# Threshold search shared between two engines: ScalarE counts the two longest tiles, in step with the projection

## The reference

```python
rel = jax.nn.relu(jnp.einsum('bthd,bsd->bths', qi, ki))
score = jnp.einsum('bths,bth->bts', rel, wi) * idx_scale
score = jnp.where(allowed[None], score, -jnp.inf)
top_val, top_idx = lax.top_k(score, topk)          # topk = 256
logits = einsum(q, k[top_idx]) * HEAD_DIM ** -0.5
p = jax.nn.softmax(logits)
out = einsum(p, v[top_idx])
```

## Time and profile before

| | |
|---|---|
| median of 3 runs | 1478.3 us |
| the profiled execution | 1476.31 us |
| its span | 1474.4 us |
| PE busy | 1288.4 us (87%) |
| DVE busy | 911.0 us (62%) |
| ACT busy | 638.5 us (43%) |
| POOL busy | 436.5 us (30%) |
| 224 counts on DVE (L1750) | 214.5 us, and 17.3 us for reading their sums |
| POOL's rows between 500 and 550 us | none |

### The profile page before, as it was taken

The page is one execution under the profiler, slowest core; times in us unless marked ns, Lnnn a source line. Parts: engine busy times, 40 slices in busy tenths (PEclk is TensorE's granted clock), DMA queues, the critical chain, the costliest instruction groups (busy, mean ns, idle before and its releaser), DMA issues.

```text
span 1474.4 us, 29883 instructions
## 1 busy us (share of the span) xinstructions
PE 1288.4 (87%) x10636; PEld 925.0 (63%) x10636; DVE 911.0 (62%) x1691; ACT 638.5 (43%) x1253; POOL 436.5 (30%) x518
## 2 busy tenths in 40 slices
PE   5968788999995336788997999999999998999997
PEld 3443334544443225566444888888888887888887
DVE  4324679999999995898655655555555553222012
ACT  3546786544156314887333444444444442101011
POOL 4772336486297100000202333333333310000001
PEclk9988999999997558999999999999999999999999
DMA  5221000102112100100531222222222128121013
GB/s 192 87 62 32 15 27 19 58 36 92 62 29 63 37 1 15 44 31 24 155 123 37 59 57 57 57 57 57 57 57 57 28 79 210 44 79 37 0 30 90
DMA packets 81594, 86.67 MB, mean 59 GB/s; under 512 B 6768, under 2 KB 63120, under 8 KB 81520
## 3 DMA queue, kind: packets, MB, share of 16 engines
q1 hardware_dynamic: 76112, 75.07, 17.8%
q10 hardware_dynamic: 4848, 8.99, 1.6%
q0 software_dynamic: 560, 1.61, 0.4%
HBM read 72.34 MB, written 13.31 MB: 58 GB/s over the span
## 4 chain that ended last, share of the span: by engine, by line
PE 51%; DVE 6%; ACT 2%; issue 2%; DMA 1%; SPq 1%; POOL 0%; POOLq 0%; DVEq 0%; ACTq 0%
PE PS L1139 28%; PE PS L1196 14%; PE PS L1102 5%; DVE M L1858 2%; DVE M L1847 2%; DMA M<-in_w_down 1%; PE PS L1022 1%; PE PS L1052 1%; PE PS L999 1%; SPq L631 1%; PE PS L1183 1%; ACT M L1454 0%; PE PS L1116 0%; ACT M L1443 0%; DVE M L425 0%
## 5 line engine op out<-in xcount | busy, mean ns | idle before, releaser
L1139 PE MATMUL PS<-M 128*128 128x264 f16 x3696 | 420.0, 277 | 9.6 <-ACT M L1562 9.6
L1139 PEld LDWEIGHTS PS<-M 128*128 128x128 f16 x3696 | 363.2, 98 | 66.0 <-ACT M L1562 10.2
L873 PE MATMUL PS<-M 128*128 128x512 f16 (+1 forms) x1512 | 305.9, 363 | 3.9 <-DVE M L425 3.6
L1196 PE MATMUL PS<-M 128*128 128x256 f16 x2112 | 233.0, 274 | 6.2 <-DVE M L2080 6.2
L873 PEld LDWEIGHTS PS<-M 128*128 128x128 f16 (+1 forms) x1512 | 138.7, 103 | 154.1 <-issue 13.8
L1196 PEld LDWEIGHTS PS<-M 128*128 (+1 forms) x2112 | 207.1, 98 | 31.7 <-issue 7.1
L1750 DVE TENSOR_SCALAR_CACHE_REDUCE M<-M,small 128x384 f16<-128x384 f32 (+6 forms) x224 | 214.5, 987 | 0.4 <-DVE small L1762 0.3
L667 POOL TENSOR_TENSOR small<-small 128x1 f32<-128x1 f32 x27 | 5.5, 203 | 543.1 <-ACT M L1509 293.7
L821 POOL TENSOR_TENSOR M<-M 128x264 f32<-128x264 f32 x44 | 34.7, 789 | 282.6 <-ACT M L1562 282.6
L2080 DVE SCALAR_TENSOR_TENSOR M<-PS,M 128x256 f32 (+1 forms) x32 | 13.6, 424 | 164.6 <-PE PS L1196 164.5
L1919 DVE SCALAR_TENSOR_TENSOR M<-M 128x2048 f16<-128x2048 f32 (+1 forms) x44 | 88.9, 2024 | 36.2 <-ACT M L1500 36.2
(11 more groups left out here) (167 smaller groups left out, 1860.3 us busy)
## 6 DMA issues: line engine op xcount, KB each, us to landing
M<-in_w_in SPq DMA_DIRECT2D x24, 512.0 KB, 4.5
M<-in_w_gate SPq DMA_DIRECT2D x22, 512.0 KB, 4.0
M<-in_w_up SPq DMA_DIRECT2D x22, 512.0 KB, 5.2
M<-in_w_down SPq DMA_DIRECT2D x20, 512.0 KB, 4.0
M<-in_x_prompt SPq DMA_DIRECT2D x16, 512.0 KB, 4.8
M<-in_w_out SPq DMA_DIRECT2D x8, 512.0 KB, 3.8
h_scratch<-M ACTq DMA_DIRECT2D x8, 512.0 KB, 5.1
M<-h_scratch SPq DMA_DIRECT2D x16, 256.0 KB, 7.3
```

Of the source, the lines that this page charges most:

```text
L873: last = pe.matmul(bank(b)[:, 0:w], xnT[:, ds(t, 1), k, s, :].squeeze(1), wt[wbuf(c)][:, k * w:(k + 1) * w], start=(k == 0 and i == 0), st ...
L1139: last = pe.matmul(o, wsp[x][:, zw, wb, k * P:(k + 1) * P], ablk[:, ab, za, k * HT + s * SC:k * HT + (s + 1) * SC], start=(name not in kep ...
L1196: last = pe.matmul(o[:, 0:256], cols[:, ds(m * SC + r * P, P)], wt[dc % 2][:, f, :], start=(f == 0 and i == 0), stop=(f == FT - 1 and i == 2))
```

## The change

Of each round's seven counts, the two of the longest tiles (7 and LAST) move to ACT. There the threshold minus the score goes through Sign, the signs are summed, and a tiny copy makes a count of the sum (`sign_count`). The first of these stands behind E, the second at the end of a step, in 31 steps: all of u, k and v and four of q. Tile 7 gets 32 more columns, filled with an inadmissible value, so that both are 1056 wide. DVE counts five tiles, waits for ACT (`act_counted`), and judges and turns bits for all seven at once; its loops become straight code, and the `piece_lo` stand singly behind rounds. Ties count half by signs, so two counts and four tiny steps at the end set these two thresholds exactly. The scratch of the masks moves to the rows that the counts dump into, and four of the seven masks follow the search at once, without waiting for q; the other three stay before jobs 1, 3 and 5.

```diff
+            def sign_count(c, t, i):
+                b = round_of(c, t)
+                j = ON_DVE + i
+                o = SC_OFF[SCORE_TILES[j]]
+                if i == 0:
+                    act.wait_ge(sel, b * SEL_ROUND + (SEL_FIRST - SEL_ROUND))
+                else:
+                    act.wait_ge(signs_summed, b * ON_ACT - 1)
+                act.activation(sign_out, scores[:, o:o + TOK], ACT.Sign, scale=-1.0, bias=kth[:, j:j + 1],
+                               accum_out=signs[:, i:i + 1]).then_inc(signs_summed, 1)
+                if i == ON_ACT - 1:
+                    act.wait_ge(signs_summed, b * ON_ACT)
+                    act.activation(cnt[:, ON_DVE:NS], signs, ACT.Copy, scale=-0.5, bias=TOK / 2).then_inc(act_counted, 1)
...
                     E(c, t, rep)
+                    if searching(c, t):
+                        sign_count(c, t, 0)
...
+                    if searching(c, t):
+                        sign_count(c, t, 1)
...
-        EARLY_MASKS = 0
+        EARLY_MASKS = 4
...
-        tie = [view(RW, oX + 4608 * i + 1024, [TOK], F16) for i in range(2)]
+        tie = [d[:, 0:TOK] for d in dump]
...
+            def bit_round(b):
+                base = SEL_FIRST + (b - 1) * SEL_ROUND
+                for j in range(ON_DVE):
+                    count(j, base + max(0, j - 1))
+                dve.wait_ge(act_counted, b)
+                judge(ALL, b, base + ON_DVE)
+                turn_bits(ALL, b + 1, base + ON_DVE + 1)
+                n_sel[0] += SEL_ROUND
...
+            for b in range(1, 32):
+                bit_round(b)
+                if b in LO_ROUNDS:
+                    piece_lo(dve, LO_ROUNDS[b])
...
+            for j in range(ON_DVE, NS):
+                o, S = SC_OFF[SCORE_TILES[j]], S_REAL[SCORE_TILES[j]]
+                link(dve.tensor_scalar(dump[j % 2][:, 0:S], scores[:, o:o + S], kth[:, j:j + 1], None, ALU.is_gt,
+                                       ALU.add, accum_out=cnt[:, j:j + 1]))
...
-            dve.wait_ge(post_evac, n_unit(NC - 1, LAST) + 2)
             for i in range(EARLY_MASKS):
                 mask(i)
+            dve.wait_ge(post_evac, n_unit(NC - 1, LAST) + 2)
```

More of the change, by code:

```diff
@@ L78 @@
     SC_OFF[_t] = _o
-    _o += S_OF[_t]
+    _o += max(S_OF[_t], TOK) if _t == LAST - 1 else S_OF[_t]
 SC_SIZE = _o
 NS = len(SCORE_TILES)
+ON_ACT = 2
+ON_DVE = NS - ON_ACT
+SURE = TOPK - 0.5
+TINY = 1.1754944e-38
+STEP = 2.0 ** -24 * (1 + 2.0 ** -10)
 ATT_TILES = [0, 1, LAST] + list(range(2, LAST))
@@ L216, in encoder_step @@
         cnt, need = tiny(8), tiny(8)
+        signs, fix = tiny(2), tiny(2)
         bits = tiny(33).bitcast(U32)
@@ L224, in encoder_step @@
         PSf = PS[:, :, :].rearrange("p a b -> p (a b)")
+        sign_out = view(RS, 8192, [TOK], F16)
+        kth = cand.bitcast(F32)
         def bank(b):
@@ L258, in encoder_step @@
         sel = sem("sel")
+        signs_summed, act_counted = sem("signs_summed"), sem("act_counted")
         mask_ready = sem("mask_ready")
@@ L376, in lagged, with round_of @@
                 part(c, t - lag, rep - lag)
+        SEL_FIRST = 2 + NS + 3 + 2
+        SEL_ROUND = ON_DVE + 2
+        def round_of(c, t):
+            return (c - cC["u"]) * NT + t + 1
         def only_vs(part):
@@ L1387, in score_relus, with searching @@
                     head(i * 2 + 1, 1, False)
+            def searching(c, t):
+                return c >= cC["u"] and (c < NC - 1 or isinstance(t, int) and round_of(c, t) < 32)
+            def sign_count(c, t, i):
[11 more added lines that the diff above has]
+                    act.activation(cnt[:, ON_DVE:NS], signs, ACT.Copy, scale=-0.5, bias=TOK / 2).then_inc(act_counted, 1)
             for c in range(NC):
@@ L1427, in step @@
                                        scale=WS).then_inc(ws_hi, 1)
-                steps(act, c, step, *LOOP[c])
+                steps(act, c, step, *((4, 8) if c == NC - 1 else LOOP[c]))
                 if c in FLUSHED:
@@ L1728, in _ @@
                 o = SC_OFF[t]
-                last = dve.memset(scores[0:CHUNK, o + S_OF[t] - CHUNK:o + S_OF[t]], INADMISSIBLE)
-            last.then_inc(sel, 1)
+                dve.memset(scores[0:CHUNK, o + S_OF[t] - CHUNK:o + S_OF[t]], INADMISSIBLE)
+            o = SC_OFF[LAST - 1]
+            dve.memset(scores[:, o + SEQ:o + TOK], INADMISSIBLE).then_inc(sel, 1)
             n_sel = [1]
@@ L1741, in link @@
                 dve.wait_ge(sel, n_sel[0])
-            kth = cand.bitcast(F32)
             def count(j, done, side=None):
@@ L1770, in _ @@
             dve.wait_ge(sel, n_sel[0])
-            link(dve.tensor_scalar(cand[:, 0:NS], cnt[:, 0:NS], TOPK - 0.5, float(0x7FFF0000), ALU.is_lt, ALU.mult))
-            link(dve.tensor_scalar(add[:, 0:NS], cnt[:, 0:NS], TOPK - 0.5, float(0xFFFF), ALU.is_lt, ALU.mult))
+            link(dve.tensor_scalar(cand[:, 0:NS], cnt[:, 0:NS], SURE, float(0x7FFF0000), ALU.is_lt, ALU.mult))
+            link(dve.tensor_scalar(add[:, 0:NS], cnt[:, 0:NS], SURE, float(0xFFFF), ALU.is_lt, ALU.mult))
             link(dve.tensor_tensor(cand[:, 0:NS], cand[:, 0:NS], add[:, 0:NS], ALU.bitwise_or))
-            SET_A, SET_B = slice(0, 4), slice(4, NS)
@@ L1776, in _ @@
-            PER = NS + 4
-            judge(SET_A, 0, n_sel[0])
-            turn_bits(SET_A, 1, n_sel[0] + 1)
+            ALL = slice(0, NS)
+            judge(ALL, 0, n_sel[0])
+            turn_bits(ALL, 1, n_sel[0] + 1)
             n_sel[0] += 2
-            dve.wait_ge(sel, n_sel[0])
[L1782 to L1795, removed]
@@ L1798, in _ @@
[L1798 to L1806, removed]
@@ L1807, in _ @@
[L1807 to L1812, removed]
+            assert n_sel[0] == SEL_FIRST
+            def bit_round(b):
[6 more added lines that the diff above has]
+                n_sel[0] += SEL_ROUND
@@ new lines, in _ @@
+            LO_ROUNDS = {round_of(c - 1, 2 + i): first_piece[c] + i for c in range(cC["k"], NC) for i in range(4)}
+            for b in range(1, 32):
+                bit_round(b)
+                if b in LO_ROUNDS:
+                    piece_lo(dve, LO_ROUNDS[b])
+            dve.wait_ge(sel, n_sel[0])
+            sure = kth[:, ON_DVE:NS]
+            link(dve.scalar_tensor_tensor(out=fix, in0=sure, scalar=-1.0, in1=sure, op0=ALU.mult, op1=ALU.max))
+            link(dve.scalar_tensor_tensor(out=sure, in0=fix, scalar=TINY, in1=sure, op0=ALU.is_ge, op1=ALU.mult))
@@ new lines, in _ @@
+            for j in range(ON_DVE, NS):
+                o, S = SC_OFF[SCORE_TILES[j]], S_REAL[SCORE_TILES[j]]
+                link(dve.tensor_scalar(dump[j % 2][:, 0:S], scores[:, o:o + S], kth[:, j:j + 1], None, ALU.is_gt,
+                                       ALU.add, accum_out=cnt[:, j:j + 1]))
+            link(dve.scalar_tensor_tensor(out=fix, in0=cnt[:, ON_DVE:NS], scalar=SURE, in1=fix, op0=ALU.is_ge,
+                                          op1=ALU.mult))
+            link(dve.scalar_tensor_tensor(out=sure, in0=fix, scalar=STEP, in1=sure, op0=ALU.mult, op1=ALU.add))
```

## The result

The changed kernel takes 1467.3 us in the median of four runs (1466.7 to 1470.1), the kernel before in the same session 1478.4: a ratio of 0.993 (95% interval 0.9913 to 0.9948). Timed a second time beside the experiments it was 0.9931 (0.9905 to 0.9956). So the change is 10 to 11 us faster, more than the 3 us that can be told; I had forecast 1479, no change.

What follows compares the result with a forecast made beforehand. PE bounds u, k and v, a POOL and ACT loop nearly equals it in q, then DVE bounds the attention's start. 1476.3 - 19.4 + 4.5 + 15.3 = 1476.7, or 1479 on the median's scale, no change; range 1465 to 1491.

Steps and rivals of the forecast that it cites:

- ScalarE's counts, to E(q,5): In projection chunks u, k, v and q: ACT's 2.75 us of counting a step costs +4.5 us (1 to 10).
- masks beside q: In chunk q: DVE's four masks take turns with POOL, which loses 16.5 us less its gaps, +15.3 (7 to 17).
- DVE's wait gone at the start: At the attention's start: the search no longer ends last, so the first exponential waits 7.0 us less.
- first exponential to packed peak: In the first attention jobs: four masks leave, 20.7 less 6.3 for exposed products and 2.0 for PE-paced jobs, gain 12.4 us.
- My lower end of 7: In q: the masks cost only 7 us if the 16-bit scan and selection don't hold POOL.
- the 6.26 of the products: At the first packed job: its 24 products, formerly beside the last mask, would become exposed, giving back 6.3 us.
- the 2.0 for jobs paced by PE: Behind the last mask: some eight jobs paced by PE at 1.2 us against DVE's 0.93, giving back 2.0 us.
- Rival 1: In q: faster, because the masks hold POOL for less than 15.3 us; 1468 us; chance 0.30.
- Rival 2: In q: slower, PE's clock stays lower as PE idles, making PE the bound; 10 us more, 1489; chance 0.18.
- rival 3: In search rounds: DVE and ACT wait for each other, half a microsecond a step, 1490 to 1495 us; chance 0.08.
- Rival 4: At the search's end: rounds lag past the end of q, so the search doesn't shorten; about 1495 us; chance 0.04.
- what I had said would show it: Signs: search end 430 to 440 us, masks 35 to 45, q step some 10, first exponential 505 to 510, peak 549 to 556.

Runs made afterwards that it cites:

- after: First profile of the changed kernel itself: profiled execution 1470.07 us, span 1468.1; the kernel's median is 1467.3 us.
- after_again: Second profile of the same changed kernel, nothing altered: span 1460.8 us; the kernel timed again gave 1467.63 us, ratio 0.9931.
- masks_as_counts: Changed kernel with each of the four early masks replaced by six counts of the search's form (masks wrong): 1459.24 us, ratio 0.9873 to the kernel before.
- kinds: Changed kernel with the four early masks replaced by five rows of one VectorE operation kind each, 768 wide, beside steps of q: single run, 1468.01 us.
- seven_early: Changed kernel with all seven masks, instead of four, straight behind the search: 1449.78 us, ratio 0.98 to the kernel before.
- search_no_signs: Shared search without early masks, with ScalarE's counts and VectorE's wait for them left out (two tiles' masks wrong): 1470.57 us, ratio 0.9954 to the kernel before.
- short_fifth_count: Changed kernel with VectorE's 896-wide count reading only 384 columns, its round 0.53 us shorter (that threshold wrong): 1462.89 us, ratio 0.9907 to the kernel before.
- search_only: Changed kernel with no early masks, all seven laced into the first jobs, so the shared search alone: 1478.45 us, ratio 0.9996 to the kernel before.
- seven_compare_summed: All seven masks straight behind the search, with the mask's comparison also summing along the row: 1447.09 us, ratio 0.9782 to the kernel before.

## Why the prediction was wrong

The change's own course, net of the offset, in the terms of the prediction, up to the first packed peak:

| term | predicted | after | after_again |
|---|---|---|---|
| ScalarE's counts, to E(q,5) | +4.5 | +4.9 | +4.4 |
| masks beside q | +15.3 | +8.5 | +8.5 |
| cached keys, memset to table load | 0 | +1.0 | 0.0 |
| DVE's wait gone at the start | -7.0 | -7.0 | -7.0 |
| first exponential to packed peak | -12.4 | -16.6 | -16.6 |
| sum | +0.4 | -9.2 | -10.7 |

**The step that failed: the masks' price in q.** I wrote that POOL "then loses the 16.5 us less its gaps", 15.3. The mechanism held: exclusive turns, and masks_as_counts shows that nothing but the kind of operation makes the price. The size did not. Each turn costs POOL the DVE operation less 0.3 us (kinds). With twenty such operations in four masks, 16.5 less 20 x 0.3 is 10.5 (9.9 without the four tiny ones of 0.15, which are in the 16.5); the rows of POOL beside the masks are 9.6 us longer together, and 8.5 of these reach the end of q. The steps of q grew to 7.8, 8.4 and 9.1 us, not to 10.4. The Trainium skill (SBUF — State Buffer, "SBUF: two separate sides") has it that whoever comes second blocks fully until the first is done. By the rows the operations do take turns, but their reported lengths overlap by about 0.3 us; over twenty turns that is 6 of the 6.8 us between 15.3 and 8.5. My lower end of 7, put down to 16-bit operations that hold nothing, was near the number for the wrong reason: comparisons and scans with 16-bit results hold POOL as any other.

**The second: what four masks give back among the jobs.** 20.7 less 16.6 leaves 4.1 us exposed, where I had 8.3. The exposed products took 4.06 us: PE was busy 7.1 of 10 us with the short jobs ahead and these products, at a granted clock of 1.00, where in the kernel before it was busy 3.0 of 10 in the same window, at 0.50 (columns as in the earlier trace rows; after's row stands above):

```profile
535.00:545.00 10.00, 3.03 (x16) 1.52 (x15) 9.28 (x16) 1.73 (x6) 0.00 (x0) 0.50 0.01 2
```

I took the 6.26 of the products in that slower window. And the 2.0 for jobs paced by PE at 1.2 us did not exist: seven_early has them at 0.8.

**ScalarE's term was right in sum and wrong in its parts.** 4.9 and 4.4 against 4.5. But u lost 3.4 instead of 1.0, k's first steps 2.5 (3.0 predicted), the scattered splits gave back 3.3 us at E(k,8) instead of 0.7 (2.9 by search_no_signs), and v's end with the first steps of q lost 2.7 to 2.9 instead of 1.2. There I had said DVE "is no longer the slow one"; short_fifth_count shows that it is. In search_only the same stretch lost more, and the term was 7.1. In ten profiles with this same search (the changed kernel's two and eight of the experiments) it is 4.4 to 5.3 in four and 6.5 to 7.1 in six, so that 4.5 was met is in part luck: it is not settled what decides between 4.4 and 7.

**The start.** The -7.0 came whole. The 1.0 us at the cached keys is a wait for a load (M<-in_cache_k, 0.89 us) in one profile and absent in the other.

**Behind the first packed peak** part of the gain may be lost again: in after one row of packed products with the values took 5.25 us at a granted clock of 0.50, in the kernel before the same 108 products 3.32.

```profile
555.00:560.00 5.00, 3.11 (x25) 2.17 (x24) 3.23 (x8) 2.07 (x5) 0.00 (x0) 0.54 0.00 0
560.00:565.00 5.00, 5.00 (x75) 4.67 (x75) 0.00 (x0) 0.00 (x0) 0.00 (x0) 0.50 0.01 3
```

```profile
561.41 5.25 PE L1068 MATMUL PS<-M 128*32 128x64 f16 x108
```

```profile
570.86 3.32 PE L1052 MATMUL PS<-M 128*32 128x64 f16 x108
```

In the second profile of the changed kernel they took 3.86 us, so two executions of one program differ by 1.4 us; in the eleven profiles of the experiments it is 3.83 to 5.27, never the 3.32 of the kernel before. At the last peak of the attention the changed kernel is 8.3 us ahead in the one profile, 10.8 in the other, net of the offset; the medians say 11.

**The rivals.** Rival 1 is what happened (1468 against 1467.3). Its mechanism, that the masks hold POOL for less, gave 6.8 us; the other 4.2 came from the jobs, which it did not have, so its number is in part luck. Its first reason, the 16-bit operations, falls with kinds: comparisons and scans with 16-bit results hold POOL. Rival 2 did not come: PE's clock was 1.00 from 440 to 458 us and 0.86 from 458 to 470, with steps of 8 to 9 us. Of rival 3 there is a little at v's end. Rival 4's search would have ended late; it ended at 434.1 us. Of what I had said would show it, the search's end and the two signs of 1.17 us a step came, and the first exponential, straight behind its table load, at 503.75 instead of 505 to 510. DVE idled for ACT's count for 35.2 us in all (12.6 in the first round alone), but in 16 of 31 rounds, not in most. The masks took 33 us instead of 35 to 45, q's step 7.8 to 9.1 instead of 10, and the packed peak came at 544, below my 549 to 556. The stretch from exponential to peak, for which I had asked 9 us, gave 16.6.

## What to carry to other kernels

Price two engines that take turns by the turn, not by the sum: each turn here cost the waiting one the other's operation less about 0.3 us, so that twenty short operations of 16 us cost 9.6. Work that only has to be done before a hand-over belongs where its engine waits for the hand-over anyway: four masks straight behind the search and four behind q were worth the same, four behind POOL's last split 6 to 7 us more, and all seven straight behind the search another 18 us over four. When half of a serial loop goes to another engine, compare the remaining half, with everything that interrupts it, with the step of its new partner; 5.4 to 5.7 against 5.1 us was enough to hold the projection by 2 to 3 us.

## What the runs showed of the hardware

- GpSimd is held by VectorE's comparisons from 32 to 16 bit, 32-bit scalings with one input and 16-bit scans; not by comparisons that sum along the row (24 of them beside GpSimd's rows of 1.27 and 0.72 us). Adding a sum to a comparison therefore frees GpSimd: beside the second mask's comparison L763 takes 1.34 us in after and 1.15 in seven_compare_summed.
- A sign with its sum over 1056 columns takes 1.17 us on ScalarE and 0.19 for the read, and adds no table load here: there are four before and four now.
- A tiny two-input operation of VectorE (L1843, 128x2) takes 0.16 us, but 1.21 when it starts 0.07 us behind a GpSimd operation of 1.26 (L1845): the loss is nearly all of GpSimd's operation, however small VectorE's own.
